# Summing the two parts of an expert product: a reduction in PSUM for a copy and an addition

## What is computed

```python
def expert_choice_ffn(h, w_router, w_gate, w_up, w_down):
    t = h.reshape(n_tok, D)
    aff = jax.nn.softmax((t @ w_router).astype(jnp.float32), axis=-1)
    cap = max(1, EC_CAPACITY * n_tok // N_EXPERTS)
    gate, idx = lax.top_k(aff.T, cap)
    xe = jnp.take(t, idx, axis=0)
    hid = jax.nn.silu(jnp.einsum("ecd,edf->ecf", xe, w_gate)) * jnp.einsum("ecd,edf->ecf", xe, w_up)
    ye = jnp.einsum("ecf,efd->ecd", hid, w_down) * gate[..., None].astype(h.dtype)
    out = jnp.zeros_like(t).at[idx.reshape(-1)].add(ye.reshape(-1, D))
```

## Time and profile before

| | |
|---|---|
| median of 3 runs | 2651.77 us (2651.76 to 2651.93) |
| span of the profiled execution | 2647.7 us |
| TensorE busy | 2414.7 us, 91% |
| VectorE busy | 1235.3 us, 47% |
| ScalarE busy | 981.3 us, 37% |
| GpSimd busy | 444.2 us, 17% |
| granted TensorE clock, mean | 0.959 |

### The profile page before, as it was taken

How to read it: one execution, slowest core, us unless ns; L and a number is a source line. 1 busy time by engine, 2 the same in 40 slices (tenths; PEclk the granted TensorE clock), 3 DMA queues, 4 the chain that set the end, 5 groups by cost and what they waited for, 6 DMA issues and landing times. The chain is left out here.

```text
span 2647.7 us, 38172 instructions
## 1 busy us (share of the span) xinstructions
PE 2414.7 (91%) x14495; PEld 2089.8 (79%) x14495; DVE 1235.3 (47%) x1813; ACT 981.3 (37%) x1644; POOL 444.2 (17%) x306
## 2 busy tenths in 40 slices
PE   5999998999799999999899798069999999999997
PEld 4876665666688888888788687069999999999997
DVE  6334345445423320000244434956666666666663
ACT  6333333434500011211300222135565555655653
POOL 0001101110200000000000000023434434344342
PEclk7999998998999999999899899579999999999998
DMA  5300000001011112222344443268788887888872
GB/s 167 104 24 25 17 24 17 17 25 40 2 47 40 40 31 83 90 89 89 104 153 146 170 159 116 90 196 257 235 257 250 261 256 233 258 249 264 254 234 64
DMA packets 328236, 342.67 MB, mean 129 GB/s; under 512 B 11856, under 2 KB 308816, under 8 KB 327632
## 3 DMA queue, kind: packets, MB, share of 16 engines
q1 hardware_dynamic: 315280, 309.96, 37.3%
q0 software_dynamic: 12864, 31.46, 4.5%
HBM read 297.35 MB, written 44.04 MB: 129 GB/s over the span
## 5 line engine op out<-in xcount | busy, mean ns | idle before, releaser
L1977 PE MATMUL bank_pair<-tokens_hi_lo,ehi 128*128 128x320 f32 x2048 | 534.0, 347 | 1.1 <-DVE tokens_hi_lo L1843 1.1
L1978 PE MATMUL bank_pair<-tokens_hi_lo,elo 128*128 128x160 f32 x2048 | 483.9, 236 | 0.0
L1978 PEld LDWEIGHTS bank_pair<-tokens_hi_lo,elo 128*128 128x128 f32 x2048 | 392.5, 192 | 0.0
L1977 PEld LDWEIGHTS bank_pair<-tokens_hi_lo,ehi 128*128 128x128 f32 x2048 | 385.7, 188 | 1.2 <-issue 1.2
L1778 ACT ACTIVATE ehi<-eraw 128x2048 fp32r<-128x2048 f32 x192 | 366.2, 1907 | 10.8 <-DMA eraw<-in_w_eg 7.9
L1836 DVE TENSOR_TENSOR elo<-eraw,ehi 128x2048 fp32r<-128x2048 f32 x144 | 329.2, 2287 | 82.7 <-ACT ehi L1778 82.7
L1754 POOL TENSOR_TENSOR elo<-eraw,ehi 128x2048 fp32r<-128x2048 f32 x47 | 224.8, 4783 | 388.2 <-ACT ehi L1778 388.2
L1977 PE MATMUL bank_pair<-hidden_hi_lo,ehi 128*128 128x320 f32 x1024 | 271.6, 348 | 19.1 <-DVE hidden_hi_lo L1849 19.1
L1978 PE MATMUL bank_pair<-hidden_hi_lo,elo 128*128 128x160 f32 x1024 | 241.4, 236 | 0.0
L1977 PEld LDWEIGHTS bank_pair<-hidden_hi_lo,ehi 128*128 128x128 f32 x1024 | 191.9, 187 | 23.4 <-DVE hidden_hi_lo L1849 22.1
L1206 PE MATMUL bank_pair<-hT_hi,whi 128*128 128x512 f32 (+1 forms) x576 | 204.0, 354 | 1.2 <-PEq L1036 1.2
(11 more groups left out here) (245 smaller groups left out, 4365.0 us busy)
## 6 DMA issues: line engine op xcount, KB each, us to landing
eraw<-in_w_eg SPq DMA_DIRECT2D x64, 1024.0 KB, 7.3
eraw<-in_w_eu SPq DMA_DIRECT2D x64, 1024.0 KB, 5.4
eraw<-in_w_ed SPq DMA_DIRECT2D x64, 1024.0 KB, 5.3
raw<-in_w_in SPq DMA_DIRECT2D x64, 512.0 KB, 4.1
scratch_g<-sig SPq DMA_DIRECT2D x24, 640.0 KB, 3.4
sig<-scratch_g SPq DMA_DIRECT2D x24, 640.0 KB, 3.9
xt<-in_x SPq DMA_DIRECT2D x10, 512.0 KB, 4.6
scratch_m<-acc SPq DMA_DIRECT2D x8, 640.0 KB, 4.9
```

The source lines that it names most:

```text
L1977: nc.tensor.matmul(out, wh, moving[:, k, :], start=(k == 0), stop=False)
L1978: ins = nc.tensor.matmul(out[:, HI], wl, moving[:, k, HI], start=False, stop=(k == KD - 1))
```

## The change

ScalarE's copy of the LO columns goes, and with it its wait for product j at the end of the step, the two `low` buffers and the semaphore `low_product_copied`. VectorE waits for product j itself (`mm5`) and takes the sum with one `tensor_reduce` over an inner axis of length 2 (the HI and the LO column of a token, 160 floats apart in PSUM), in w_down's products with two of them. Nothing else is changed; the order of what stays is the same on every engine. Lines behind L1640 have other numbers in the changed kernel.

```diff
--- before.py
+++ after.py
@@ -1637,7 +1637,6 @@
     xp = place("tokens_hi_lo", [P, KD, 2 * CAP], F32R)
     hid = place("hidden_hi_lo", [P, KD, 2 * CAP], F32R)
     HI, LO = slice(0, CAP), slice(CAP, 2 * CAP)
-    low = [place(f"low_product{i}", [P, 2, CAP]) for i in range(2)]
     gate_sum = place("gate_sum", [P, 2, CAP])
     up_sum = place("up_sum", [P, 2, CAP])
     sg = place("silu_gate", [P, 2, CAP])
@@ -1679,7 +1678,6 @@
     h_ready = sem("hidden_ready")
     h_hi = sem("hidden_hi")
     h_lo = sem("hidden_lo")
-    low_ready = sem("low_product_copied")
     summed = sem("product_summed")
     y_tr = sem("y_rows_transposed")
     y_rdy = sem("y_rows_ready")
@@ -1817,9 +1815,6 @@
                         x_split(e + 1, 2)
                     if before and j in (1, 2):
                         y_out(e - 1, j - 1)
-                    act.wait_ge(mm5, c + 1)
-                    wait(act, summed, c - 1)
-                    nc.scalar.activation(low[j % 2][:], pairs[j % 2][:, :, LO], ACT.Copy).then_inc(low_ready, 1)
 
             for j in range(AHEAD):
                 hi(0, j)
@@ -1888,21 +1883,18 @@
                     if after and j == 11:
                         x_split(e + 1, 2)
 
-                    dve.wait_ge(low_ready, c + 1)
+                    dve.wait_ge(mm5, c + 1)
                     q = 4 * e + j // 2
-                    src, m = pairs[j % 2], 2 * (j - 8)
+                    src, m = pairs[j % 2][:, :, 0:2 * CAP].rearrange("p m (h t) -> p m t h", h=2), 2 * (j - 8)
                     if j >= 8:
                         if j == 8:
                             wait(dve, y_tr, 2 * e)
-                        nc.vector.tensor_tensor(yT_s[:, m:m + 2, :], src[:, :, 0:CAP_S], low[j % 2][:, :, 0:CAP_S],
-                                                ALU.add)
-                        ins = nc.vector.tensor_tensor(yT_p[:, m:m + 2, :], src[:, :, CAP_S:CAP],
-                                                      low[j % 2][:, :, CAP_S:CAP], ALU.add)
+                        nc.vector.tensor_reduce(yT_s[:, m:m + 2, :], src[:, :, 0:CAP_S, :], AX.X, ALU.add)
+                        ins = nc.vector.tensor_reduce(yT_p[:, m:m + 2, :], src[:, :, CAP_S:CAP, :], AX.X, ALU.add)
                     else:
 
                         wait(dve, silu_ready if j % 2 == 0 else h_ready, q)
-                        ins = nc.vector.tensor_tensor((gate_sum, up_sum)[j % 2][:], src[:, :, HI], low[j % 2][:],
-                                                      ALU.add)
+                        ins = nc.vector.tensor_reduce((gate_sum, up_sum)[j % 2][:], src, AX.X, ALU.add)
                     ins.then_inc(summed, 1)
                     if j < 8 and j % 2 == 1:
                         dve.wait_ge(summed, c + 1)

```

## The result

The changed kernel takes 2627.76 us in the median of four executions (2627.34 to 2628.52), the kernel before 2651.77 (2649.40 to 2651.93). The ratio is 0.991, 95% interval 0.9896 to 0.9924: 24.0 us faster. One execution of the kernel before, of 5866.23 us in a slow state beside ten of 2649 to 2653, is left out of these ratios.

What follows compares the result with a forecast made beforehand. TensorE was taken as the bound. The gain, 16 x 1.19 - 16 x 0.1 + 0.1 = 17.5 us, off the 2647.7 us span gave 2630.2; with 4.1 added, 2634.3 us, range 2632 to 2661.

Steps and rivals of the forecast that it cites:

- These 19.1 us are all that a change of the summing can win in this stage: Expert stage: TensorE's 16 waits for hidden_lo in product 8, 1.19 us idle each, were the whole possible gain.
- I leave 0.1 us per expert for the error of these hand-offs: Allowance for errors in engine-to-engine start times before product 8, taken off the gain: 16 x 0.1 us.
- the forecast's own road: Predicted chain up to product 8's waiting matmul, which may go on at 2061.61 to 2061.82, against 2061.83 wanted.
- the median of the runs is 2651.8, 4.1 above the span: Offset of 4.1 us added to turn the predicted span, 2630.2 us, into the predicted median, 2634.3.
- The price of the reduction: VectorE's 640-element sum was taken at 0.82 us, from reductions of neighbouring elements; 1.37 was the upper price.
- the dear row: Profile row of a 128-element VectorE copy writing SBUF at a step of four floats, 0.38 us; basis for 1.37 us.
- The road to ehi of chunk 11: Chain from product 1's sum to ScalarE's conversion of weight chunk 11, forecast to start at 2053.60 instead of 2055.01.
- The cover over VectorE's extra work: TensorE takes 4.1 us per product and needs each sum only before product j+2, hiding VectorE's extra 66 us.
- The strided rival: Reading pairs 160 floats apart makes VectorE's reduction 1.37 us, so waits grow 4 to 8 us: 2658; chance 0.33.
- break-even: Reduction length of 1.22 to 1.29 us at which TensorE's gap is back at 1.19; above that the change loses.
- The half gap: GpSimd's subtraction of chunk 7 does not move; gap stays 0.4 to 0.6 us, gain 10 to 13: 2641; chance 0.12.
- No unlocking: Something else, such as late raw weights, holds ScalarE's ehi of chunk 11; only 0.1 us won: 2651.7; chance 0.10.

Runs made afterwards that it cites:

- The probes: Changed kernel with eleven, then six more VectorE instructions behind its last work; 256-element reductions with tokens 4 floats apart took 0.63 us from SBUF, 0.42 from PSUM.
- the longer sum: Changed kernel with a spare 0.40 us VectorE copy out of PSUM ahead of each gate and up reduction: 2642.23 us, ratio 0.9962.
- the wait kept: Changed kernel, but ScalarE still waits for product j at the end of step j, copying nothing: 2646.21 us, ratio 0.9981.

## Why the prediction was right and wrong

- **"These 19.1 us are all that a change of the summing can win in this stage"**: this step failed. The sum was made with 1.19 us per expert, the idle time as the profile counts it from the modelled end of a matmul; measured is 1.43, from start to start. 16 x 0.24 = 3.8 us of the miss. For the same reason the matmul was wanted at 2061.66 and not at 2061.83.
- **"I leave 0.1 us per expert for the error of these hand-offs"**: not needed, 1.6 us, but this was in part luck. With the due time of 2061.66 the forecast's own road (2061.61 to 2061.82) would have left a gap of up to 0.16 us. It closed with 0.26 us to spare (2002.50 against 2002.76) because GpSimd was done 0.2 to 0.4 us sooner than forecast, for a reason that the forecast did not have.
- **"the median of the runs is 2651.8, 4.1 above the span"**: the profiled execution itself took 2649.4 us, 1.7 above its span, and was 2.4 below the median of the runs. This offset falls out of the forecast, which is 2651.8 - 17.5. In the traces the stage explains 23.0 of the 24.0 us between the medians; the last 1.0 is within what executions differ by.
- **The price of the reduction**, 0.82 us against 1.37: right, 0.820 to 0.822. So were those of 512 and 128 elements, 0.69 and 0.28 against 0.69 and 0.29. The probes show why the dear row misled: its 0.38 us is SBUF's, not PSUM's. The page of the Trainium skill that I held against the change (Advanced Engine Details and Errata, PSUM Cachelines) does not hold for VectorE's reads here: partners 160 floats apart take 0.81 us, neighbours 0.82. Its section also speaks of matmuls, which no run here tests.
- **The road to ehi of chunk 11**, put on the clock of the after trace by the end of product 7: y_rows_p 1.91 us behind product 1 forecast, 1.95 measured; "hidden" of quarter 2 at -6.05, measured -6.33; ehi at -5.15, measured -5.43; GpSimd's end at +1.42 to +1.63, measured +1.21. The 0.2 to 0.3 us by which all this is ahead of the forecast (of its earlier value, for GpSimd) come from one place: GpSimd's first scatter of prompt rows took 1.86 us instead of 2.12, and so chunk 7's subtraction let "hidden" of quarter 1 go 0.87 us sooner, not 0.6. The forecast moved this scatter by its start. The traces show its end to follow VectorE's subtraction of chunk 5 instead: before, that one ends at 2038.52 and the scatter at 2039.96, after, at 1978.76 and 1980.20, both times 1.44 us later, and within 0.02 us of that in four other experts of either trace. That subtraction came 0.86 us sooner.
- **The cover over VectorE's extra work held**: no wait of TensorE for a sum. But the load was put too high, at 40 us of 55: the window has 37.42, and over the stage VectorE's busy time grew from 565.9 to 589.2 us, 23 and not 66. The forecast left out that "hidden", held for less time, counts 37 us less as busy (100.4 to 63.0).
- **The strided rival** had its mechanism right, as the longer sum shows: at 1.22 us it is 14.5 us slower than the change. But its break-even was put at 1.22 to 1.29 us, and at 1.22 there are still 9 us of gain: GpSimd is done 2.41 us behind product 7 there, in the kernel before 2.83. At three times the length the other 0.42 make 0.14 us, so that an estimate from these two rows puts the break-even at some 1.36 us. **The half gap** (a second GpSimd stretch that doesn't move) did not come: it moved by more than 0.6. **No unlocking** did not come either; the wait kept is nearest to that case, and it costs 18 us.
- **Not foreseen**: the low clock in some executions. It was seen only in kernels whose gap is closed, but of the kernel before, the wait kept and the longer sum there is one profile each, so it is not shown that the gap keeps it away.

## What to carry to other kernels

When an engine copies something for another, look at what stands behind the copy in its program: here 84 us of copies were worth nothing by themselves, and one copy, with its wait, that stood ahead of the conversion of one weight chunk cost 23 us. Follow a gap of the bounding engine back over every engine, GpSimd's hold on two-input VectorE instructions included, until it reaches a wait that needn't be there; moving one instruction may do. Price a gap in a pipelined engine from the start that was due to the start that came, not by its idle time.

## What the runs showed of the hardware

- VectorE reads PSUM at the same pace at every step tried: 128 elements take 0.29 us at steps of 1, 2, 4 and 8 floats. In SBUF a step of 2 floats is free and one of 4 costs 0.09 us on 128 elements, reading or writing; the reduction of 256 elements goes from 0.42 to 0.63.
- A reduction costs by its inputs, in the shapes seen: out of 512 inputs, 256 results of 2 take 688 ns and 2 results of 256 take 691; 320 results of 2, out of 640, take 820.
- With a GpSimd subtraction running, a multiplication with two inputs in SBUF ends 0.35 to 0.37 us behind it, whatever its own start; reductions and additions with one input in PSUM run through it. A GpSimd scatter that overlaps a VectorE subtraction with two inputs in SBUF ends 1.44 us behind that, whether it takes 1.86 or 2.12 us: this fits a hold the other way round, which no run tests by itself.
- Where TensorE had no gap: in two profiled executions of the changed kernel seven dips to a granted clock of 0.50 each, the two followed closely some 3.3 us long and behind 2.6 us of transposes, 1.6 us dear in the mean; no long execution in eight with the transposes in shorter stretches.
- A gap of TensorE costs more than its idle time in the profile, which is counted from a modelled end: 1.43 us for 1.19, 1.09 for 0.88, 0.96 for 0.73.
